# Half the frequencies in a long convolution, its projection started per block, and right-hand sides of a triangular inverse written one group earlier

## The reference, cut to what matters

```
u = (short_conv(z, conv_w, n_seg, seg_len) + conv_b)
v, x1, x2 = jnp.split(u, 3, axis=-1)
filt_f = jnp.fft.rfft(filt, axis=0)
y = v
for o, gate in enumerate((x1, x2)):
    conv = jnp.fft.irfft(jnp.fft.rfft(y, n=2 * l, axis=1) * filt_f[None, :, o], n=2 * l, axis=1)[:, :l]
    y = gate * (conv + d_skip[o] * y)
```

## Time and profile before

| | us |
|---|---|
| median of 3 runs | 2426.66 (2421.22 to 2435.16) |
| the profiled execution's own time | 2422.91 |
| span of its trace | 2420.8 |
| TensorE busy | 2268.8 |
| VectorE busy | 1386.1 |
| GpSimd busy | 1120.0 |
| ScalarE busy | 583.9 |
| mean granted TensorE clock | 0.967 |

### The profile page before, as it was taken

The page is one execution under the profiler, slowest core; times in us unless marked ns, Lnnn a source line. Parts: engine busy times, 40 slices in busy tenths (PEclk is TensorE's granted clock), DMA queues, the critical chain, the costliest instruction groups (busy, mean ns, idle before and its releaser), DMA issues.

```text
span 2420.8 us, 34156 instructions
## 1 busy us (share of the span) xinstructions
PE 2268.8 (94%) x14122; PEld 1835.8 (76%) x14122; DVE 1386.1 (57%) x1983; ACT 583.9 (24%) x1199; POOL 1120.0 (46%) x642
## 2 busy tenths in 40 slices
PE   7999899999899999899999999998988988999998
PEld 5777687887776777777788757587888966788886
DVE  4445678567644444567947855286865774630532
ACT  2043222022123222222012132044544222210210
POOL 4520465765643221466766533053420055656654
PEclk9999999999999999899999999998999999999999
DMA  4210223433511110233433541021210012223322
GB/s 167 83 53 10 70 94 119 163 96 109 200 61 52 44 45 18 70 96 101 155 115 106 200 179 53 0 70 45 88 36 3 4 54 78 83 92 96 105 87 70
DMA packets 55001, 203.84 MB, mean 84 GB/s; under 512 B 6176, under 2 KB 6432, under 8 KB 53568
## 3 DMA queue, kind: packets, MB, share of 16 engines
q1 hardware_dynamic: 52272, 187.28, 23.4%
q0 software_dynamic: 1840, 11.70, 1.3%
q10 hardware_dynamic: 736, 2.69, 0.3%
HBM read 197.45 MB, written 4.19 MB: 83 GB/s over the span
## 4 chain that ended last, share of the span: by engine, by line
PE 87%; DVE 6%; ACT 3%; POOL 2%; issue 1%; DMA 0%; DVEq 0%; SPq 0%; POOLq 0%; ACTq 0%
PE bank L524 65%; PE bank L944 3%; PE bank L972 2%; PE bank L1552 1%; PE bank L1560 1%; PE bank L959 1%; PE bank L2341 1%; POOL parts_r L505 1%; PE bank L1530 1%; PE bank L648 1%; PE bank L2337 1%; PE bank L948 1%; PE bank L2608 1%; PE bank L2326 1%; POOL parts_r L499 1%
## 5 line engine op out<-in xcount | busy, mean ns | idle before, releaser
L524 PE MATMUL bank<-xn_r,parts_r 128*128 128x512 f32 (+1 forms) x2928 | 921.5, 393 | 32.7 <-DVE mix_r L725 13.9
L524 PE MATMUL bank<-big_r,parts_r 128*128 128x512 f32 x3208 | 935.7, 394 | 16.4 <-DVE big L888 8.9
L499 POOL TENSOR_SCALAR parts_r<-ring 128x1024 fp32r<-128x1024 f32 x293 | 336.1, 1147 | 1045.4 <-PE bank L524 1037.6
L505 POOL TENSOR_TENSOR parts_r<-ring,parts_r 128x1024 fp32r<-128x1024 f32 x293 | 733.3, 2503 | 24.4
L524 PEld LDWEIGHTS bank<-big_r,parts_r 128*128 128x128 f32 x3208 | 605.6, 190 | 149.6 <-DVE big L888 10.6
L524 PEld LDWEIGHTS bank<-xn_r,parts_r 128*128 128x128 f32 x2928 | 553.6, 191 | 152.3 <-issue 32.2
L851 ACT ACTIVATE big<-bank,small 128x512 f32<-128x512 f32 x88 | 68.3, 778 | 419.7 <-DVE big L895 251.2
L880 DVE TENSOR_TENSOR bank<-bank,nb 128x512 f32<-128x512 f32 x88 | 61.3, 699 | 148.9 <-PE bank L524 148.9
L2949 DVE TENSOR_TENSOR big<-big 128x512 f32<-128x512 f32 x32 | 82.6, 2584 | 70.9 <-ACT big_r L2930 70.9
L2875 DVE SCALAR_TENSOR_TENSOR h<-bank,vecs,h 128x512 f32<-128x512 f32 x24 | 17.9, 750 | 173.1 <-PE bank L524 173.1
L535 DVE TENSOR_TENSOR big_r<-big,big_r 128x512 fp32r<-128x512 f32 x76 | 105.6, 1392 | 0.4
(11 more groups left out here) (409 smaller groups left out, 2893.6 us busy)
## 6 DMA issues: line engine op xcount, KB each, us to landing
ring<-weights SPq DMA_DIRECT2D x295, 512.0 KB, 3.5
cst<-mod_w SPq DMA_DIRECT2D x48, 512.0 KB, 4.3
big<-consts POOLq DMA_DIRECT2D x3, 1024.0 KB, 8.2
cst<-consts SPq DMA_DIRECT2D x2, 1280.0 KB, 9.1
h<-x SPq DMA_DIRECT2D x8, 256.0 KB, 6.6
h_store<-h POOLq DMA_DIRECT2D x8, 256.0 KB, 2.3
big<-consts POOLq DMA_DIRECT2D x1, 2048.0 KB, 14.3
h<-h_store POOLq DMA_DIRECT2D x1, 2048.0 KB, 9.0
```

The source lines that it names most:

```text
L499: pool.tensor_scalar(rounded(unit_parts(u)[0]), ring[:, u % RING], 1.0, 0.0, ALU.mult, ALU.add)\
L505: pool.tensor_tensor(rounded(lo), ring[:, u % RING], value(hi), ALU.subtract).then_inc(part_ready, 1)
L524: mm = pe.matmul(ps, rounded(w[a]), rounded(x[b]), start=(start and n == 0), stop=(stop and n == 2))
```

## The change

Positions are reordered, even tokens first, then odd ones (`order`). With NFREQ = 256 the cosine and sine tables cover half the frequencies; even and odd positions are transformed apart, and their sum and difference give the lower and the upper half. So a filter spectrum is made of eight products over two position tiles each, and VectorE's `filter_halves` adds and subtracts. In the convolutions the unit is one half of the channels (m) of one order (o), u = 2o + m: `hyena_turn`, `hyena_spectrum`, `hyena_product`, `hyena_back`, `hyena_gate`.

The first two projection chunks are made block by block as `x2al` counts up, ahead of `mod_pe`; their taps come ahead of the context's squares on ScalarE and of its reciprocal on VectorE. The `ag` projection moves among the convolutions, into banks 6 and 7, and `decay_gates` behind the second query chunk. Right-hand sides 3, 4 and 5 get buffers of their own in `h` and are written in group 0, behind its levels 1, 2 and 3. GpSimd loads half of each table (dft), ScalarE half of the cosines.

The diff, cut; removed bodies are those printed above:

```diff
-NFREQ = T
+NFREQ = T // 2
 AG = {"gla_f": 0, "gla_b": 32, "decay": 64, "beta": 96}
...
-    n = np.arange(T)
-    w = np.outer(n, 2 * np.arange(NFREQ) + 1) % (4 * T) * (np.pi / (2 * T))
+    order = np.concatenate([np.arange(0, T, 2), np.arange(1, T, 2)])
+    w = np.outer(order, 2 * np.arange(NFREQ) + 1) % (4 * T) * (np.pi / (2 * T))
...
-                filter_spectrum_pe(pe, 0, (2, 3))
-                for i, ks in enumerate(((0, 1), (2, 3), (4, 5, 6, 7))):
-                    filter_spectrum_pe(pe, i + 1, range(TB))
-                    for k in ks:
-                        sum_squares(pe, "ffn1n", k)
+                filter_spectrum_pe(pe, 1)
+                for k in range(KD):
+                    sum_squares(pe, "ffn1n", k)
+                    if k in SPECTRUM_AT:
+                        filter_spectrum_pe(pe, *SPECTRUM_AT[k])
                 for i in range(TB, 2 * TB):
-                    filter_spectrum_pe(pe, i, range(TB))
+                    filter_spectrum_pe(pe, i)
...
+            hyena_conv(dve, 0)
+            hyena_conv(dve, 1)
...
-        dft = [part(2048 * n, TB, T) for n in range(4)]
+        dft, idft = [part(2048 * n, TB, NFREQ) for n in range(2)], [part(4096 + 1024 * n, 2, T) for n in range(2)]
...
+        H_even = part(6144, 4, T)
+        by_parity = lambda a: a.rearrange("p (s two) -> p two s", two=2)
+        yT = [part(14336 + n * T, TB, P) for n in range(2)]
+        U_odd, UU = part(1024, 2, T), part(3072, 2, T)
+        both = lambda a: big[:, a:a + 2 * T].rearrange("p (q c n) -> p q c n", q=4, c=2)
+        UU4, A4, B4, Y4 = both(3072), both(10240), both(15360), both(16384)
+        Ysum = part(16384, 2, T)
+        Yt = [part(6144 + 2 * T * n, 2, T) for n in range(2)]
+        HY_COPY = {("yT", 0): 1, ("yT", 1): 2, ("odd", 0): 3, ("odd", 1): 4,
+                   ("yT", 2): 5, ("odd", 2): 6, ("yT", 3): 7, ("odd", 3): 8}
+        hy_copied = lambda what, u: after("yT", HY_COPY[what, u])
...
+        SPECTRUM_AT = {1: (2, (0,)), 3: (2, (1,)), 5: (3, (0,)), 6: (3, (1,))}
...
+            c, ft, par = i // 4, i // 2 % 2, i % 2
+            if halves[0] == 0:
                 if i == 0:
                     pe.wait_ge(*after("f_sum", 4 * TB))
                     pe.wait_ge(sem("cos_in"), 16)
-                if i == TB:
+                if i == 4:
                     pe.wait_ge(sem("sin_in"), 16)
                 grab(pe, i % 4, *after("H", i + 1))
-            for pt in pts:
+            for n in halves:
+                pt = 2 * par + n
                 mm = pe.matmul(bank[i % 4][:, :], (dft_cos, dft[1])[c][:, pt, ft * P:(ft + 1) * P], (hsum, hdif)[c][:, pt],
-                               start=(pt == 0), stop=(pt == TB - 1))
-            if pts[-1] == TB - 1:
+                               start=(n == 0), stop=(n == 1))
+            if halves[-1] == 1:
                 mm.then_inc(sem("H_ps"), 1)
+        def hyena_turn(pe, u):
+            o, m = divmod(u, 2)
+            pe.wait_ge(*after("hy_y" if o else "hy_u", m + 1 if o else 6))
+            ps = grab(pe, 4 + m, *hy_copied("yT", u))
+            src = u_hy[:, m].rearrange("p (h s two) -> p two h s", h=2, two=2)
+            for pt in range(TB):
+                mm = pe.transpose(ps[:, pt * P:(pt + 1) * P], src[:, pt // 2, pt % 2], ident)
+            mm.then_inc(sem("y_turn"), 1)
+        def hyena_spectrum(pe, u):
+            m = u % 2
+            pe.wait_ge(*hy_copied("yT", u))
+            odd = grab(pe, 2 * m + 1, *hy_copied("odd", u))
+            even = grab(pe, 2 * m, *after("spec", 2 * u + 1))
+            for ps, pts in ((odd, (2, 3)), (even, (0, 1))):
+                for q in range(4):
+                    ft, c = divmod(q, 2)
+                    for pt in pts:
+                        mm = pe.matmul(ps[:, q * P:(q + 1) * P], dft[c][:, pt, ft * P:(ft + 1) * P], yT[m][:, pt],
+                                       start=(pt == pts[0]), stop=(pt == pts[1]))
+                mm.then_inc(sem("U"), 1)
+        def hyena_back(pe, u):
+            m = u % 2
+            pe.wait_ge(*after("Y", 2 * u + 2))
+            ps = grab(pe, 4 + m, *after("hy_y", u + 1))
+            for par in range(2):
+                for q in range(4):
+                    ft, c = divmod(q, 2)
+                    mm = pe.matmul(ps[:, par * 2 * P:(par + 1) * 2 * P], Yt[m][:, par, q * P:(q + 1) * P],
+                                   idft[c][:, ft, par * 2 * P:(par + 1) * 2 * P], start=(q == 0), stop=(q == 3))
+            mm.then_inc(sem("conv"), 1)
+        def ag_product(pe, p, ks):
+            rhs, n = (lat, ctxp)[p]
+            if ks[0] == 0:
+                if p == 0:
+                    take(pe, UNITS["ag"])
+                else:
+                    pe.wait_ge(*after("x2bl", KD))
+                grab(pe, 6 + p, *after("ag", p + 1))
+            for k in ks:
+                mm = hi_lo_product(pe, bank[6 + p][:, 0:n], weight(UNITS["ag"], slice(k * P, (k + 1) * P)), rhs(k),
+                                   k == 0, k == KD - 1)
+            if ks[-1] == KD - 1:
+                mm.then_inc(sem("ag_ps"), 1)
+            if p:
+                product_done[UNITS["ag"]] = after("ag_ps", 2)
+        def hyena_first_pe(pe):
+            u0 = UNITS["hy"]
+            two = [grab(pe, f, *after("hy_u", f + 1)) for f in range(2)]
+            for k in range(KD):
+                pe.wait_ge(*after("x2al", k + 1))
+                for f, ps in enumerate(two):
+                    if k == 0:
+                        take(pe, u0 + f)
+                    mm = hi_lo_product(pe, ps[:, :], weight(u0 + f, slice(k * P, (k + 1) * P)), lat[0](k), k == 0, k == KD - 1)
+                    if k == KD - 1:
+                        mm.then_inc(sem("hy_ps"), 1)
+                    product_done[u0 + f] = after("hy_ps", f + 1)
         def hyena_pe(pe):
-            fm_multi(pe, "hy", 6, [lat], "hy_ps", "hy_u")
+            hyena_first_pe(pe)
+            mod_pe(pe)
+            fm_multi(pe, "hy", 6, [lat], "hy_ps", "hy_u", first=2)
             pe.wait_ge(sem("dft_in"), 32)
...
+            early, late = range(KD // 2), range(KD // 2, KD)
+            hyena_turn(pe, 0)
+            hyena_turn(pe, 1)
+            hyena_spectrum(pe, 0)
+            hyena_spectrum(pe, 1)
+            ag_product(pe, 0, early)
+            hyena_back(pe, 0)
+            ag_product(pe, 0, late)
+            hyena_back(pe, 1)
+            for u in (2, 3):
+                hyena_turn(pe, u)
+                hyena_spectrum(pe, u)
+            hyena_back(pe, 2)
+            ag_product(pe, 1, range(KD))
+            hyena_back(pe, 3)
...
         def filter_act(act):
-            for i in range(TB):
+            for i in range(TB + 2):
                 filter_take_act(act, i)
-            for i in range(TB):
-                x2_act(act, 2 * i)
-                x2_act(act, 2 * i + 1)
-                filter_take_act(act, TB + i)
+            for k in range(KD):
+                x2_act(act, k)
+                if k < 2:
+                    filter_take_act(act, TB + 2 + k)
...
+            for what, u in sorted(HY_COPY, key=HY_COPY.get):
+                m = u % 2
+                if what == "yT":
+                    act.wait_ge(*after("y_turn", u + 1))
+                    dst, src = yT[m].rearrange("p k n -> p (k n)"), bank[4 + m]
+                else:
+                    act.wait_ge(*after("U", 2 * u + 1))
+                    dst, src = U_odd[:, m], bank[2 * m + 1]
+                act.activation(dst, src[:, :], ACT.Copy).then_inc(sem("yT"), 1)
...
+        def filter_halves(dve, upper, c):
+            for ft in range(2):
+                even, odd = H_even[:, 2 * c + ft], (Hc, Hs)[c][:, 2 + ft]
+                dst = odd if upper else (Hc, Hs)[c][:, ft]
+                ins = dve.tensor_tensor(dst, even, odd, ALU.subtract if upper else ALU.add)
+            if c and not upper:
+                link(dve, ins)
+        def hyena_product(dve, u):
+            o, m = divmod(u, 2)
+            H4 = [a[:, :, o * HY_C + m * P:o * HY_C + (m + 1) * P].unsqueeze(2).broadcast_to((P, 4, 2, P)) for a in (Hc, Hs)]
+            dve.wait_ge(*hy_copied("odd", u))
+            dve.wait_ge(*after("U", 2 * u + 2))
+            dve.tensor_tensor(UU[:, 0], bank[2 * m][:, :], U_odd[:, m], ALU.add)
+            dve.tensor_tensor(UU[:, 1], bank[2 * m][:, :], U_odd[:, m], ALU.subtract).then_inc(sem("spec"), 1)
+            dve.wait_ge(*after("spec", 2 * u + 1))
+            dve.tensor_tensor(A4, UU4, H4[0], ALU.mult)
+            dve.tensor_tensor(B4, UU4, H4[1], ALU.mult).then_inc(sem("spec"), 1)
+            dve.wait_ge(*after("spec", 2 * u + 2))
+            dve.tensor_tensor(Y4[:, :, 0], A4[:, :, 0], B4[:, :, 1], ALU.subtract)
+            dve.tensor_tensor(Y4[:, :, 1], B4[:, :, 0], A4[:, :, 1], ALU.add).then_inc(sem("Y"), 1)
+            dve.wait_ge(*after("Y", 2 * u + 1))
+            dve.tensor_tensor(Yt[m][:, 0], Ysum[:, 0], Ysum[:, 1], ALU.add)
```

(55 more changed lines are left out.)

110 lines of the change are left out of this document (30 added, 80 removed).

## The result

| | kernel before | changed kernel |
|---|---|---|
| time, median | 2425.45 us (2421.22 to 2435.16, 4 runs) | 2391.16 us (2387.64 to 2395.83, 4 runs) |
| profiled execution, span | 2420.8 us | 2385.8 us |
| mean granted clock | 0.967 | 0.964 |

The ratio is 0.9854, 95% interval 0.9818 to 0.989: 34 to 35 us saved, where 46.7 were forecast and 2378 us stood as the time. The page answers the earlier trace rows: VectorE and the holes have grown in the chain.

A forecast was written before the change was run, and what follows sets the result against it. TensorE was taken to bound the kernel (busy 94% of the span, 87% of the chain). Terms -9.7 - 33.0 + 1 - 5 = -46.7 us gave 2378 us, own range 2369 to 2389 (0.60), stated range 2366 to 2394.

The forecast's parts named there:

- part 2: Convolutions and ag: half the columns and ag hidden under VectorE's products, 46.7 us for 79.7, -33.0 (bounds -38 to -19).
- parts 1: Filter's spectrum and start of the mixer: 32 records for 64, but TensorE waits for VectorE; net -9.7 (-12 to -7).
- 4: Inverse: right sides 3, 4, 5 no longer wait, 7 us saved, 2 lost in group 0; -5 (-7.5 to +1).
- slow VectorE: Rival, convolutions: broadcast and paired patterns run at half speed, 4 units x 3 us, 2390 us; chance 0.12.
- part 3: Gates: decay_gates behind gl_q's second chunk makes the gl_v copies late for TensorE by 1.8; +1 (0 to +4).
- Meeting one split less: Mixer start: VectorE's context work, from 1455.4, meets one GpSimd split fewer and ends at 1466.
- The last step: Mixer start: after the context work, VectorE's four convolutions and eight adds or subtractions run from 1466 to 1481.5.
- a hole over 8: Sign of being wrong: TensorE idle over 8 us before the first turn; a wait of 4.9 was forecast.
- The slack of 7.68: Gates: VectorE idle 7.68 us before it was needed; a chain starting 5.4 us later leaves 2.3.
- The rival that put 15 to 20 us here: Rival, gates: VectorE's chain starts late, slack is used up, gates hold 15 to 20 us back; 2396 us, chance 0.04.
- the inverse gives nothing: Rival, inverse: clock stays slow between groups and ScalarE's copies bound the steps; 2383 to 2385 us, chance 0.13.
- slower than before: the clock: Rival: TensorE granted 1.2 GHz through convolutions and gates, +68 us net, 2495 us; chance 0.03.

The follow-up runs named there:

- second pair: The kernel before and the changed kernel each profiled again, code unaltered, one execution each: 2420.61 and 2376.07 us.
- Experiment 3: Changed kernel with VectorE's filter halves moved behind the split of X2 and behind the first two convolutions: 2386.19 us, 0.9845.
- experiment 7: Changed kernel with the products of ag behind the convolutions' last return instead of among them: 2403.41 us, 0.9912.
- 10: Changed kernel with two of the eight operations of hyena_product done twice: turn to gl_q 52.57 us for 45.28, whole profile 2400.44 us.
- 5: Changed kernel with decay_gates, and ScalarE's exponential, behind gl_q's first chunk instead of the second: 2387.95 us, 0.9854; gates 77.84 us for 81.68.
- 12: Changed kernel, code unaltered, profiled a second time: 2376.07 us, one execution.
- 4: Changed kernel with the right sides behind the attention products in group 0, not ahead: 2385.88 us, 0.9851; group 0 73.92 us for 76.71.
- experiment 1: Kernel before with only the inverse's part of the change (right sides 3, 4, 5 written in group 0): 2425.5 us, 0.9997.
- experiment 9: Changed kernel with filter halves and decay_gates moved as in Experiment 3 and 5, but the inverse as before the change: 2385.6 us, 0.981.
- first pair: The first profiles of the kernel before and of the changed kernel: spans 2420.8 and 2385.8 us.

## Why the prediction was right, and where it missed

The direction held, and part 2 is by far the greatest, as forecast; parts 1 and 4 changed places. The time, 2391.16, lies in the stated range of 2366 to 2394, but 2.2 us past my own of 2369 to 2389. It is next to the 2390 of *slow VectorE*, whose mechanism did not occur, so that the time stayed within the range is partly luck. The sum was too large by 12 us: by part 1 most of all, by part 3, and by what stages with unchanged code did.

- **Part 1, -9.7 forecast, -3.8 measured, -4.7 in the second pair.** The spectrum's own 13.8 came. The failing steps are VectorE's beside GpSimd. The base of the whole profile lies 1.3 earlier, so against the forecast the reciprocal of X2 started 1.2 late (1430.06 for 1430.2) and that of the context 2.3 (1456.38 for 1455.4). The first 1.2 stand behind 3.4 us at the lower clock near 1415; the second profile has none there, and its L1530 to first product is 0.9 shorter. The other 1.0 is TensorE's wait of 1.02: L1452 and L1457 took 2.25 and 2.83 beside GpSimd's subtraction, which I had not put there. "Meeting one split less" was then wrong: the context work took 14.3 us, as long as before the change, and ended 6.0 late. The last step, 15.5 us from there to the last tap, measured 15.4. I had the backlog and a hole of 4.9; it was 8.59, and a hole over 8 was one of my signs of being wrong. The last tap ended at 1486.09, past my outer bound of 1484, and the term fell outside its bounds of -12 to -7: they varied the taps' stretch and left the context work ahead of it fixed. Experiment 3 took 5.4 of the hole away.
- **Part 2, -33.0 forecast, -34.1 and -35.2 measured.** A product is 6.35 us on VectorE (1493.74 to 1500.09), as worked out; the 1024s took 1.23, so broadcast and paired patterns cost nothing, and the rival *slow VectorE* is out. 128 columns cost 0.12, near the floor of 0.109. The first spectrum ran slow, once (0.59, then 1.00). TensorE's idle was 3.07, at the edge of the 3 that I named, and the clock granted over the stage 0.94. `ag` was free (experiment 7), VectorE the longer half (10). The first chunk of gl_q began at 1531.47 and not near 1525: 4.6 of this are part 1's, the rest is the slow first spectrum, which the 1525 left out.
- **Part 3, +1 forecast, +3.2 and +3.0 measured**, inside its bounds. The path by the copies of gl_v was right and its size was not: TensorE waited 3.15 and 3.50 us for them, where I had 1.8, and its waits for GpSimd fell from 1.7 to 0.1 and 1.1. In the first profile 3.4 us more at the lower clock did the rest. The slack of 7.68 was read on another path: it is VectorE's idle in the next stage, and it is 7.68 again in the second profile. The failing step is the length of the chain through VectorE and ScalarE ahead of the copies, which the later place alone brought into TensorE's way (5 and 12). The rival that put 15 to 20 us here was the right place at the wrong price.
- **Part 4, -5 forecast, -5.7 and -4.8 measured.** The transition gave 9.9 for 7, because its 13.7 us at the lower clock went as well (0 in the first profile, 3.4 in the second). That is partly luck: in experiments 7 and 10 the same code ran 13.7 and 10.2 us at the lower clock and took 22.42 and 20.72, a gain of 4.7 and 6.4. Group 0 cost 4.2 for 2: the delay at levels 2 and 3 was 0.94 each as forecast, but it costs more than once, as the stretches at the lower clock behind it grew from 10.2 to 17.1 us, and with the attention products in front 2.8 of it went (4). The rival *the inverse gives nothing* had the wrong mechanism for these stages, but the whole time looks like it (experiment 1), and experiment 9 does not decide.
- **The sum.** The parts' own error is 6.4 us in the first pair, 5.1 in the second. The rest of the first pair, 5.3, is unchanged code at another clock, and the second pair has 2.7 the other way; why the medians stay at 34 to 35 is open. The prediction allowed for this only as a slow kernel (*slower than before: the clock*), never as a few microseconds of either sign per stage.

**A rule of the Trainium skill.** The long operations are one form: VectorE with two operands in SBUF, beside GpSimd's subtraction (L1714 at 3.49 and 3.79 for two, against 1.28; the scans 11.75 beside two subtractions, against 9.66 beside one), while the taps, which read one operand from a bank, took 0.73 to 0.74 wherever they stood. The Trainium skill's page SBUF — State Buffer (Who interferes with whom) says that VectorE with two SBUF inputs contends with a GpSimd instruction that reads SBUF, and with at most one, outside its 2-port modes, does not. The trace agrees with both.

## What to carry to other kernels

When TensorE's work is cut, write out VectorE's queue up to the new first wait, with every GpSimd instruction beside it: VectorE's two-operand work stretches there. Put what is needed late where the queue has slack, not ahead of what TensorE waits for (a gain of 35 us became 50 by three such moves together). Compare stages between fixed records, and more than one profile of each kernel, before a few microseconds are put down to a change.

## What the hardware showed that was not expected

- TensorE's work in unchanged code differed by 6.1 us in 1335 (start to L1530) and by 4.8 in 411 (out2 to the end) between executions, mostly with the time at the lower clock level, while the other engines repeated within 0.5%.
- A wait of 3 us in TensorE can cost more than itself: with 8.8 us of products taken out of such waits the stage took 10.3 us more, as its last return ran in part at the lower level (5.41 for 3.66).
- VectorE's stretch beside one subtraction of GpSimd is 2.2 to 2.5 us for a pair of 512-column operations (3.49 and 3.79 against 1.28), and GpSimd's own instruction grew too (2.81 against 2.44).
